# Group norm of the state-space branch: squares added on GpSimd, one product with ones per group, sums one step of side work later

## What is computed

```
y = y.reshape(b, s, SSM_INNER) * jax.nn.silu(z)          # end of branch a
return grouped_rms_norm(y, norm_w, SSM_GROUPS)           # 4 groups of 256 channels

yf = y.reshape(b, s, groups, d // groups)
yf = yf * lax.rsqrt(jnp.mean(yf * yf, axis=-1, keepdims=True) + NORM_EPS)

branch = jnp.einsum('bsiw,iwd->bsid', ys, w_proj[layer])
merged = jnp.sum(g * branch, axis=2)
```

## Time and profile before

| | |
|---|---|
| median of 3 runs | 2065.08 us (2065.0 to 2071.91) |
| profiled execution, its own time | 2065.3 us |
| its span, from the first to the last instruction | 2063.6 us |
| TensorE busy | 2043.2 us, 99% |
| weight loads (PEld) busy | 1827.8 us, 89% |
| VectorE busy | 1365.1 us, 66% |
| ScalarE busy | 1100.2 us, 53% |
| GpSimd busy | 68.7 us, 3% |
| mean granted TensorE clock | 0.997 |

### The profile page before, as it was taken

One profiled execution on the slowest core, in us unless ns is written; L12 is line 12 of the kernel. 1 busy time (PEld: TensorE's weight loads), 2 busy tenths in 40 slices (PEclk: granted clock), 3 DMA queues, 4 the chain that ended last, 5 costly groups with the idle time before them and its releaser, 6 DMA issues.

```text
span 2063.6 us, 36368 instructions
## 1 busy us (share of the span) xinstructions
PE 2043.2 (99%) x14742; PEld 1827.8 (89%) x14742; DVE 1365.1 (66%) x2356; ACT 1100.2 (53%) x1839; POOL 68.7 (3%) x55
## 2 busy tenths in 40 slices
PE   9999999999999999999999999999999999999998
PEld 9999999999999999997677887778788888999998
DVE  6687767567787786574565345665555667668786
ACT  5576685545676785453475233433332347645554
POOL 2210000000300000000000000000000000000000
PEclk9999999999999999999999999999999999999999
DMA  7556545566656535563223434433333343454552
GB/s 285 181 162 211 188 144 183 185 222 229 227 177 194 194 124 200 199 243 136 84 72 113 143 133 173 143 115 131 113 133 133 112 158 116 148 174 164 185 179 78
DMA packets 97351, 334.43 MB, mean 162 GB/s; under 512 B 11552, under 2 KB 16160, under 8 KB 96928
## 3 DMA queue, kind: packets, MB, share of 16 engines
q1 hardware_dynamic: 97184, 332.10, 47.4%
HBM read 326.94 MB, written 1.18 MB: 159 GB/s over the span
## 4 chain that ended last, share of the span: by engine, by line
PE 92%; DVE 4%; ACT 2%; issue 1%; DVEq 0%; ACTq 0%
PE ps L961 25%; PE ps L962 25%; PE ps L963 24%; PE ps L1044 2%; PE ps L974 2%; PE ps L975 2%; PE ps L976 2%; DVE t_lo L1686 1%; PE ps L1261 1%; ACT t_hi L1356 1%; PE ps L1117 1%; PE ps L1271 1%; PE ps L1282 1%; PE ps L983 1%; PE ps L1133 1%
## 5 line engine op out<-in xcount | busy, mean ns | idle before, releaser
L961 PE MATMUL ps<-t_RB,t_hi 128*128 128x256 f32 (+1 forms) x3712 | 1160.8, 313 | 4.0 <-ACT t_MT L1402 1.4
L962 PE MATMUL ps<-t_RB,t_hi 128*128 128x256 f32 (+1 forms) x3712 | 1144.4, 308 | 0.0
L963 PE MATMUL ps<-t_RB,t_lo 128*128 128x256 f32 (+1 forms) x3712 | 1144.0, 308 | 0.0
L1686 DVE TENSOR_TENSOR t_lo<-t_raw,t_hi 128x1024 fp32r<-128x1024 f32 (+1 forms) x503 | 610.7, 1229 | 363.4 <-ACT t_hi L1356 362.1
L961 PEld LDWEIGHTS ps<-t_RB,t_hi 128*128 128x128 f32 x3712 | 707.9, 191 | 73.5 <-issue 23.1
L963 PEld LDWEIGHTS ps<-t_RB,t_lo 128*128 128x128 f32 x3712 | 708.2, 191 | 35.3
L962 PEld LDWEIGHTS ps<-t_RB,t_hi 128*128 128x128 f32 x3712 | 708.4, 191 | 33.0
L1356 ACT ACTIVATE t_hi<-t_raw 128x1024 fp32r<-128x1024 f32 (+1 forms) x506 | 519.4, 1041 | 371.7 <-PE ps L963 349.4
L2126 DVE SCALAR_TENSOR_TENSOR t_A<-ps,t_V,t_A 128x510 f32<-128x510 f32 (+1 forms) x176 | 102.1, 611 | 89.0 <-ACT t_A L1646 87.4
L1646 ACT ACTIVATE t_A<-ps,t_V 128x512 f32<-128x512 f32 (+1 forms) x88 | 48.4, 576 | 127.0 <-PE ps L963 127.0
L2099 DVE SCALAR_TENSOR_TENSOR t_X<-ps,t_MOD,t_X 128x256 f32<-128x256 f32 x168 | 72.6, 477 | 32.9 <-PE ps L963 32.9
(11 more groups left out here) (308 smaller groups left out, 1869.9 us busy)
## 6 DMA issues: line engine op xcount, KB each, us to landing
t_raw<-in_W SPq DMA_DIRECT2D x586, 512.0 KB, 3.9
t_A<-cu_scratch SPq DMA_DIRECT2D x8, 512.0 KB, 6.1
t_B<-cu_scratch SPq DMA_DIRECT2D x8, 512.0 KB, 5.8
t_raw<-in_W SPq DMA_DIRECT2D x16, 256.0 KB, 3.2
t_A<-in_C SPq DMA_DIRECT2D x2, 1536.0 KB, 6.6
t_A<-t_T SPq DMA_DIRECT2D x40, 64.0 KB, 4.4
t_A<-t_T SPq DMA_DIRECT2D x40, 32.0 KB, 1.9
t_X<-in_X SPq DMA_DIRECT2D x2, 512.0 KB, 4.3
```

The source lines that it names most:

```text
L961: mm(o, hi[:, w], xh(k), start=k == 0 and j == 0, stop=False)
L962: mm(o, hi[:, w], xl(k), start=False, stop=False)
L963: i = mm(o, lo[:, w], xh(k), start=False, stop=k == nkt - 1 and m == u.x[1] - 1)
L1686: tt(t.lo[s][:, 0:w], t.raw[r][:, 0:w], t.hi[s][:, 0:w].bitcast(F), ALU.subtract).then_inc(*up("dve", ("split", u.i)))
```

## The change

Three edits, in both layers of the first model. GpSimd gets a new unit `zsq`: it waits for ScalarE's squares and adds the second block to the first in place. `gn_sum` waits for that addition and makes one product with ones in place of two. The generator `gnorm` gets one more `yield` at its start, so sums, root, reciprocals and splits all stand one step of side work later.

```diff
     def gnorm(self, l):
+        yield
         yield
         for c in range(4):
             self.add("gn_sum", l=l, c=c, g=(self.bank(),))
@@
     def gn_sum(u):
-        q.wait_ge(at("ysq", u.l, u.c))
-        b = gbank(u)
-        for m in range(2):
-            i = mm(b[:, 0:256], t.ones, t.zh(u.c % 2)[:, m, :], start=m == 0, stop=m == 1)
+        q.wait_ge(at("zadd", u.l, u.c))
+        i = mm(gbank(u)[:, 0:256], t.ones, t.zh(u.c % 2)[:, 0, :], start=True, stop=True)
         i.then_inc(*up("pe", ("gsum", u.l, u.c), ("nt", *half_of[u.l, u.c])))
@@
-    todo = dict(split=split, fox_prep=fox_prep, ssm0=ssm0, ssm2=ssm2)
+    def zsq(u):
+        zh = t.zh(u.c % 2)
+        q.wait_ge(at("ysq", u.l, u.c))
+        tt(zh[:, 0, :], zh[:, 0, :], zh[:, 1, :], ALU.add).then_inc(*up("pool", ("zadd", u.l, u.c)))
+
+    todo = dict(split=split, fox_prep=fox_prep, ssm0=ssm0, ssm2=ssm2, zsq=zsq)
```

## The result

The changed kernel took 2088.61 us (median of 4 runs, 2088.03 to 2090.86) against 2065.34 for the kernel before. The ratio is 1.0112, with a 95% interval of 1.0100 to 1.0124: slower by 23 us. The forecast was 2088.0, in a range of 2079 to 2093.

A forecast was written before the change was run, and what follows sets the result against it. TensorE's queue was taken as the bound, with VectorE late at `proj(0)`: 2065.3 - 3.4 + 11.3 + 11.6 + 3.4 = 2088.2 us, the median's forecast being 2088.0, range 2079 to 2093.

The forecast's parts named there:

- The bound: Whole kernel: TensorE, busy 99% of the span, sets the time; VectorE is already late around `proj(0)` of branch a.
- VectorE's queue: Instructions up to `YL` of groups 0 and 2, added row by row: `proj(0)` loses 11.3 and 11.6 us by layer.
- The gap: VectorE idle from 300.85 to 309.64, 8.8 us, ahead of a weight piece's `t_lo`, until ScalarE's copy is there.
- the first wait: TensorE ahead of `proj(0)` of branch a, waiting for `YL` of group 0: about 3 us, once a layer.
- The second wait: TensorE ahead of the fifth block of `proj(0)`, waiting for `YL` of group 2: 8.45 us in the first layer.
- The clock: TensorE's granted clock after the long wait in `proj(0)`: falls, costing 1.7 us a layer, 3.4 us in all.
- two such rows: Upper bound of a layer's clock cost: twice the 1.7 us lost at 1665 to 1670 of the earlier trace.
- The saving: Sums on TensorE's queue: one product less in each of eight sums, 0.43 us each, 3.4 us in all.
- GpSimd's addition: Eight additions of 128x256 on GpSimd: 0.7 us each, ends 0 and 1.42; no cost to TensorE expected.
- The cover: About 10 us between the first square's end and its later sum hide the addition; without it, 5.6 us in all.
- ScalarE's held gate: ScalarE's queue at the gate of `z(2)` and `z(3)`, held some 2 us: cost 0, other end 2 us a layer.

The follow-up runs named there:

- delay_only: The kernel before with only the extra `yield`: two products per sum, nothing on GpSimd; 2092.16 us (1.0128).
- root_with_sum: The changed kernel with one `yield` less, so the root is taken in the step of the fourth sum; 2061.55 us (0.9981).
- root_back: The changed kernel with the root in the step of the fourth sum, while `gn` and `YL` stay late; 2085.7 us.
- waits_filled: The changed kernel with idle products of TensorE put into the two waits of `proj(0)` of branch a; 2085.64 us (1.0092).
- halved_only: The changed kernel without the extra `yield`: additions on GpSimd, one product per sum, everything at its old step; 2069.6 us (1.0017).

## Why the prediction was right

**The bound.** It read TensorE's queue as the time and VectorE as the late one at `proj(0)`. `delay_only` and `root_with_sum` bear both out.

**VectorE's queue** was the largest term and came out to the hundredth. The gap was put at 8.8 us and is 8.82. From the first `t_lo` to `YL` of group 0 the working had 15.59 us; the rows have 323.56 - 307.97 = 15.59. From there to `YL` of group 2 it had 11.41; the rows have 334.97 - 323.56 = 11.41. In the time frame of after, 1.77 us earlier, `proj(0)` was to start at 324.39 and the fifth block at 335.80; they start at 324.30 and 335.71. In the second layer, 9.78 us later, the fifth block was to start at 793.35 + 9.78 = 803.13 and starts at 803.03. The nearest rows were the same instructions on the same data, and a queue that is never idle only adds up.

**The second wait** was put at 8.45 us, and under 7 us was to mean mis-sized; it is 6.95 and 7.11. Still, the lateness was not mis-sized, the test was badly put: the clock had already fallen in the first wait, so the four blocks between took 328.76 - 324.30 = 4.46 us in place of 2.96, and 1.5 us of the wait went into them. `YL` came when it was expected, and where the clock held through the first half the wait is as long as forecast: 8.60 us in the second layer of `delay_only`, 8.27 and 8.61 us in `root_back`.

**The clock** was the term that was mis-sized. I took 1.7 us a layer from the earlier trace rows. In the second halves it cost 5.38 - 2.96 = 2.42 us and 5.42 - 2.96 = 2.46, so 4.9 in place of 3.4 us, within the bounds given. Without it the two products lost 13.66 - 2.42 = 11.24 and 14.00 - 2.46 = 11.54 us, for 11.3 and 11.6 forecast. In the first halves it cost nothing, since TensorE had to wait anyway. `waits_filled` shows the price by itself, 4.64 us. The prediction left open, between 0 and two such rows, whether it would fall at all; by the Trainium skill ("TensorE: Matmul & The Clock Gate", Part 1) it was certain behind such a wait. The rows agree: behind the waits of 6.95, 7.11 and 8.60 us the clock is 0.50. Behind short waits the rows differ: after 2.52 us in the changed kernel's second layer it fell (0.66 from 790 to 795), after 2.53 us in that of `delay_only` it held.

**The saving** was put at 3.4 us. TensorE came to `proj(0)` 1.77 us earlier in the first layer and 11.89 - 9.78 = 2.11 in the second, in sum 3.88: besides the products, a wait of 0.28 us for a square in the second layer went.

**GpSimd's addition** was put at 0.7 us with 1.42 as its end. The eight take 1.22 us in the mean and 1.78 at most, beyond that end. The cover held: the changed kernel's TensorE waits for none of them, and without the cover, in `halved_only`, they cost 5.7 us, where the prediction had 5.6. That these two agree is luck: the prediction had eight waits of 0.7 us, and there were six of 0.95 in the mean. **ScalarE's held gate** was taken at 0, with 4 us in both layers as the other end; `root_with_sum`, which holds it just as long, leaves no room for such a cost.

**What the sum left out:** from the end of the second layer's `proj(0)` to the end of the execution the lag shrinks from 23.78 to 22.68 us. 0.96 of these come between 916 and 929, where the clock of the kernel before fell. Two stretches at the same place in the program, of before and, 23 us later, of after:

```profile
917.00:922.00 5.00, 4.19 (x26) 3.74 (x26) 4.00 (x10) 1.56 (x4) 0.00 (x0) 0.66 0.99 408
```

```profile
940.00:945.00 5.00, 4.20 (x42) 3.27 (x42) 3.95 (x9) 1.77 (x6) 0.00 (x0) 1.00 0.99 403
```

TensorE is busy for 4.2 us in both, and the clock is 0.66 in the one and 1.00 in the other.

The books close: -1.77 + 13.66 - 2.11 + 14.00 - 1.10 = 22.68, and the spans differ by 22.6. That the forecast lies only 0.6 us below the median (and its sum, 2088.2, 0.2 us above the profiled execution, 2088.03) owes something to errors that cancel, and that is luck: the clock was taken 1.5 us too low, the saving 0.5 us too low, and 1.1 us of give-back were not foreseen.

## What to carry over

A step that is moved takes everything behind it along on every engine: here a saving of 3.4 us on the busiest engine came with a delay on two others that cost 27.7 us (4.9 of them through TensorE's clock), and moving only the sums kept the saving. Add up, row by row, the queue of the engine that is late at the place in question, and ask for each piece whether its inputs will be there too. Averages (VectorE at 66%) say nothing about such a place.

## What I had not expected of the hardware

**The same addition on GpSimd takes 0.73 to 1.78 us, with what VectorE runs beside it.** The timelines of VectorE and GpSimd in the changed kernel, two of the eight additions beside what VectorE ran:

```profile
267.85 1.22 DVE L1685 TENSOR_TENSOR t_lo<-t_raw,t_hi 128x1024 fp32r<-128x1024 f32 x1
267.89 1.78 POOL L2193 TENSOR_TENSOR t_NT<-t_NT 128x256 f32<-128x256 f32 x1 [8.03 <-ACT t_NT L1506]
...
272.46 1.22 DVE L1846 TENSOR_TENSOR t_B<-t_B,t_ST 128x1024 f32<-128x1024 f32 x1
273.60 0.48 DVE L1804 CUSTOM_DVE_ANT_0 t_B<-ps,t_C,t_V 128x256 f32<-128x256 f32 x1
273.54 0.74 POOL L2193 TENSOR_TENSOR t_NT<-t_NT 128x256 f32<-128x256 f32 x1 [3.88 <-ACT t_NT L1506]
```

Beside a `t_lo`, which reads two operands from SBUF, the addition ends 0.60 us after the `t_lo` does (267.89 + 1.78 = 269.67 against 267.85 + 1.22 = 269.07), however early it started: the six that meet a `t_lo` take 1.26 to 1.78 us and all end 0.59 to 0.61 us after it. The two short ones, 0.74 and 0.73 us, run beside the maxima, but began 0.14 us before the end of a product of VectorE's that also reads two operands (L1846), and they too end 0.60 and 0.59 us after it (273.54 + 0.74 = 274.28 against 272.46 + 1.22 = 273.68). So it seems to stand still as long as such an instruction of VectorE runs, and to need some 0.6 us behind it. The Trainium skill, "SBUF — State Buffer", Terms, says that VectorE and GpSimd share a pair of ports that one of them holds for a whole instruction while the other is blocked; the rows agree. The other way round, a `t_lo` that starts at 283.44, while an addition runs (282.53 to 283.79), takes 1.44 us in place of 1.22. No run here changed only VectorE's part, so the cause is read from rows, not shown by an experiment.

**The clock also falls where nothing was changed.** The two stretches above, 917 to 922 of before and 940 to 945 of after, lie at the same place of the program and have 0.66 and 1.00. So it is with the place from which the forecast took its price: behind a wait of 1.03 us in both, the kernel before has 0.66 and the changed one 1.00 (1688 to 1693). Between runs of one kernel such falls come and go too: the four runs of `waits_filled` have a mean clock of 0.996 to 0.999 and 2087.01 to 2083.56 us, the least clock with the longest time. What sets them off here the runs don't tell; a difference of 2 us between two kernels can be that alone, if only a few runs stand behind it.
